# Six gather buffers instead of eight, and a piece and a half of the query weights kept on chip, in a decoder step with PEER experts on one Trainium2 core

## Chip, cores and metric

One NeuronCore of a Trainium2 chip runs the whole program. The metric is the device time of one execution in microseconds, lower is better. A run is one execution; the time before is the median of three.

## What is computed

One layer of a hybrid decoder for 512 prompt tokens and 8 sample tokens (one new token for each of 8 running sequences): modulated RMSNorm, one input projection, a gated delta net (8 heads) beside a forgetting attention (8 heads, for the samples over 2,048 cached positions), an output projection, and then PEER, a mixture of 16,384 tiny experts. Everything is fp32. The part around the change is PEER, cut to what matters:

```python
def one(xb):                                     # xb: normed tokens
    q = (xb @ wq).reshape(blk, 8, 2, 128)        # wq: 1024 x 2048
    s = einsum('thpc,hpnc->thpn', q, subkeys)    # 2 x 128 scores per head
    sv, si = top_k(s, 16)
    cand = sv[:, :, 0, :, None] + sv[:, :, 1, None, :]
    fv, fi = top_k(cand.reshape(blk, 8, 256), 16)
    eidx = ...                                   # 16 experts per token and head
    gate = softmax(fv)
    act = gelu(einsum('thkd,td->thk', pu[eidx], xb)) * gate
    return einsum('thk,thkd->td', act, pv[eidx])
```

Each token thus needs 8 heads x 16 experts, and each expert is a row of 1,024 numbers of `peer_u` and one of `peer_v`. The host lays both side by side as `peer_uv`, rows of 2,048 numbers (8 KB).

## The kernel before, in words

The prompt is cut into 4 tiles of 128 tokens. The first 568 us compute projections, attention, the sample caches and the delta net of tile 0. Then the PEER stage begins and lasts to the end. It is a stream of 520 steps (list `steps_`): 4 tiles x 8 heads x 16 experts, and 8 steps for the samples. A unit is 16 steps, that is one head of one tile.

**One step.** GpSimd (`gather(g)`, line 2650) issues an indirect DMA that fetches for each of 128 tokens its expert's 8 KB row: 128 x 8,192 bytes = 1.0486 MB into buffer `UV[g % UN]`. VectorE (`dot(g)`, line 2386) multiplies the u half with the token's row and sums it (L2398). For two steps at a time, ScalarE makes the gelu (L1476), scales it by the gate (L1482) and writes two 32-column diagonal matrices (L1466), and TensorE (`value_pair`, line 1130) adds the v halves with eight matmuls of 128x512 (L510, `bank<-RING,R` or `bank<-R`). The last matmuls raise `v_used`, one for each step of the pair.

**Landing buffers.** `UV` (line 209) has 8 buffers of 8 KB per partition: six in `RING`, buffer 6 in `R1` from column 12288, buffer 7 in `R2` from column 8192. `gather(g)` waits for `v_used` of step g - 8 (line 2661), and GpSimd does nothing else in this stage; so a buffer is asked for again when TensorE is through with it. A gather into `R1` or `R2` shows in the profile as `R<-in_peer_uv,R`, one into `RING` as `RING<-in_peer_uv,R`.

**The other work of the stage.** While tile i's experts are fetched, the delta net, output projection, norm and queries of tile i + 1 are computed, cut into pieces that are dealt out over the steps (`slots_at`, `post_slots`, `delta_slots`, lines 427 to 464). TensorE does, at each step, first the value pair (even steps), then the pieces of that step. VectorE does first the dot, then a piece of the picking of the best experts for a later unit, then the pieces of the step.

**The query weights.** `wq` is cut into 4 pieces `c` of 512 columns, 2 MB each, stored as 8 row blocks `k` of 128 rows. A piece's lower half is `k` 0 to 3, its upper half 4 to 7. Lower half of piece 0 stays on chip in `WR[0]` (`R1` from 4224). Upper half of piece 0 is kept for tile 0 in `WR[1]` (in `MV`, which holds the token rows later) and is loaded again for tiles 1 to 3. All other weights come through two slots `W[0]`, `W[1]` (`R2` 0 to 8192) in the order of the list `w_parts` (line 414); `weights_in(m)` (line 2886) loads part m when part m - 2 has been used. A tile after the first takes two pieces of the output projection (2 MB each), half of piece 0 (1 MB) and pieces 1 to 3 (2 MB each). SyncE issues these loads on its own queue, in the order in which its program comes to them.

**Before the first gather.** SyncE waits for the delta net of tile 0 (`dS`, 0), loads shift and scale of the norm (`SH2`, `SC2`, in `R2` from 8192), waits for the last attention result (`pt`, 7), and loads the sub-keys (`KN`) and `WR[1]`. VectorE needs `SC2` at L2265, TensorE needs sub-keys and both `WR` from L517 and L510 on (`keys_in`).

Of the kernel before, what the change touches and what calls it, by code (L numbers as in the profile page):

```python
# [56 lines left out]
def hybrid_decoder_step(nc, a, o):  # L57

    ctx = ExitStack()
    with ctx:  # L60
        sems = {}

        def S(name):
            if name not in sems:
                sems[name] = ctx.enter_context(nc.semaphore(name))
            return sems[name]
# [18 lines left out]
        MV = sb("MV", [P, 4, D_MODEL])  # L85
        RQ64 = sb("RQ64", [P, 328])
        R1 = sb("R1", [P, 14336])
# [3 lines left out]
        def part(_t, _at, _n, /, **dims):  # L91
            v = _t[:, _at:_at + _n]
            if not dims:
                return v
            names = list(dims)
            return v.rearrange(f"row ({' '.join(names)}) -> row {' '.join(names)}", **{k: dims[k] for k in names[1:]})
# [83 lines left out]
        W_ROWS = [part(R2, n * 4096, 4096) for n in range(2)]  # L180
        QT = part(R1, 0, 16 * (P + NB), b=16, t=P + NB)
        KEYT = part(R1, 2176, 2048, b=16, n=P)
        SH2, SC2 = part(R2, 8192, 1024), part(R2, 9216, 1024)
        SCS = HT[0:NB, :, 0:2 * P]
        ROWS, SHIFT, SCALE, GATE2, GAIN = HT[64:68, :, 0:P], 0, 1, 2, 3
        GAINS = HT[0:NB, :, 0:P]
# [19 lines left out]
        XS1 = part(R2, 13676, 1024)  # L206
        KN = part(SLOT2, 0, 2048, b=16, c=P)
        FLAT = RING[:, :, :].rearrange("p s n -> p (s n)")
        UV = [part(FLAT, i * 2048, 2048) for i in range(6)] + [part(R1, 12288, 2048), part(R2, 8192, 2048)]
        WR = [part(R1, 4224, 2048, k=4, n=512), MV[:, 0:2, :].rearrange("p n d -> p (n d)").rearrange("p (k n) -> p k n", k=4)]  # L210
        HN = part(R2, 10240, 1024)
        QUARTER = [MV[:, b, :] for b in range(4)]
        WR_ROWS = [part(R1, 4224, 2048), MV[:, 0:2, :].rearrange("p n d -> p (n d)")]
        UN = len(UV)
        FOLD = hide_q[:, 0:32]
        SX = part(R1, 10368, 256, p=2, n=P)
# [130 lines left out]
        def job_done(eng, job):  # L347

            b, use = job_of[job]
            eng.wait_ge(S(f"bank{b}_full"), use)  # L350
# [62 lines left out]

        w_parts = [(0, "wq", c) for c in range(1, 4)]
        for tile in range(1, TILES):
            w_parts += [(tile, "wo", c) for c in range(2)] + [(tile, "wq", c) for c in range(4)]

        def w_slot(eng, i, name, c):

            m = w_parts.index((i, name, c))  # L420
            eng.wait_ge(S(f"w{m % 2}_loaded"), 16 * (m // 2 + 1))
            return W[m % 2]
# [85 lines left out]
        def _(pe):  # L508
# [480 lines left out]
            def query_part(i, c, j, w, ks):  # L989

                n = P if i < TILES - 1 else P + NB
                job = ("qT", i, c, j)
                if ks[0] == 0:
                    take_bank(job, "D")
                b = banks[job_of[job][0]]
                for k in ks:
                    wk = w[:, k, :] if c else WR[0][:, k, :] if k < 4 else (w if i else WR[1])[:, k - 4, :]
                    mm(b[:, 0:n], wk[:, j * P:(j + 1) * P], HT[:, k, i * P:i * P + n], k == 0, k == KT - 1, full(job) if k == KT - 1 else None)

            def scores(i, c):  # L1000
# [76 lines left out]
            def post_slot(i, kind, c=0, j=0, q=0):  # L1077

                if kind == "rest" and c in (0, 1):
                    spread(("shift" if c else "scale", i), SHIFT if c else SCALE)  # L1080
                elif kind == "wo":
                    if c == q == 0:
                        for half in range(2 if j < 4 else 1):
                            job_read(pe, ("oT", j, half))
                        if j == 4:
                            pe.wait_ge(S("sample_attention"), 1)
                    w = w_slot(pe, i, "wo", c) if q == 0 else W[w_parts.index((i, "wo", c)) % 2]
                    mix_part(j, c, w, range(2 * q, 2 * q + 2))
                elif kind == "turn":
                    second_turn(c, j)  # L1090
                elif kind == "wq":
                    if c == j == q == 0:
                        for t in rows_of(i):
                            for half in range(2):
                                job_read(pe, ("h2T", t, half))
                    w = w_slot(pe, i, "wq", c) if j == q == 0 else W[w_parts.index((i, "wq", c)) % 2]
                    query_part(i, c, j, w, range(4 * q, 4 * q + 4))
                elif kind == "score":
                    scores(i, c)
                elif kind == "pairs":  # L1100
                    pair_turns(i, c)
                elif kind == "decay":
                    decay(i, c)
                elif kind == "product":
                    products(i, c)
                elif kind == "solve":
                    solve(i, j, c)
                elif kind in ("X", "Y"):
                    correct(i, j, c, kind)
                elif kind == "wt":  # L1110
                    state_keys(i)
                elif kind == "vn":
                    state_values(i)
                elif kind == "o":
                    state_out(i)
                elif kind == "dS":
                    state_step(i)
                elif kind == "oT":
                    out_turn(i, 0)
# [1555 lines left out]
        def _(sp):  # L2675
            def load(dst, src, sem, **k):
                sp.dma_start(dst, src, **k).then_inc(S(sem), 16)
# [208 lines left out]
            def weights_in(m):  # L2886

                i, name, c = w_parts[m]
                if m >= 2:
                    pi, pname, pc = w_parts[m - 2]  # L2890
                    job_done(sp, ("qT", pi, pc, 3) if pname == "wq" else ("wo", pc, rows_of(pi)[-1]))
                if name == "wq" and c == 0:
                    load(W_ROWS[m % 2][:, 0:2048], wq[0, :, 2048:4096], f"w{m % 2}_loaded")
                else:
                    load(W_ROWS[m % 2], {"wo": w_out, "wq": wq}[name][c], f"w{m % 2}_loaded")

# [3 lines left out]
            sp.wait_ge(S("spilled"), 32 * (TILES - LATE))  # L2900
            load(WR_ROWS[0], wq[0, :, 0:2048], "keys_in")
            job_done(sp, ("dS", 0))
            for i, dst in enumerate((SH2, SC2)):
                load(dst, mod_d[0:1, (3 + i) * D_MODEL:(4 + i) * D_MODEL].to_broadcast([P, D_MODEL]), "mv2_in")
            job_done(sp, ("pt", 7))
            load(KN, a["peer_subkeys"][0].rearrange("h p n c -> n (h p) c"), "keys_in")
            load(WR_ROWS[1], wq[0, :, 2048:4096], "keys_in")
            weights_in(0)
            weights_in(1)
            sp.wait_ge(S("gdn_out"), 1)  # L2910
# [5 lines left out]
            def post_slot(i, kind, c=0, j=0, q=0):  # L2916

                if kind == "wo" and j == rows_of(i)[-1] and q == 3:
                    weights_in(w_parts.index((i, "wo", c)) + 2)
                elif kind == "wq" and j == 3 and q == 1:  # L2920
                    m = w_parts.index((i, "wq", c)) + 2
                    if m < len(w_parts) and (w_parts[m][0] == i or w_parts[m][0] < LATE):
                        weights_in(m)
                elif kind == "tokens" and i == 1 and c == 0:
                    job_done(sp, ("qT", 0, 3, 3))
                    load(ROWS[0:3], mod_d[0:1, 3 * D_MODEL:6 * D_MODEL].rearrange("o (r k c) -> (o r) k c", r=3, k=KT), "rows_in")
                    load(ROWS[3:4], a["final_norm_w"].rearrange("(o k c) -> o k c", o=1, k=KT), "rows_in")
                elif kind == "dS":
                    job_done(sp, ("dS", i))
                    for c in range(2):  # L2930
                        weights_in(w_parts.index((i, "wo", c)))
                elif kind == "oT":
                    job_done(sp, ("oT", i, 0))
                    if i + 1 < TILES:
                        late_in(i + 1)
                    else:
                        load(G1S[0:NB], mod_d[1:9, 2 * D_MODEL:3 * D_MODEL], "g1_in")
                        tile_in(4)
                        for x, dst in enumerate((SH2S, SC2S)):
                            load(dst, mod_d[1:9, (3 + x) * D_MODEL:(4 + x) * D_MODEL].rearrange("b (k c) -> b k c", k=KT), "mv2_in")  # L2940
                        sp.wait_ge(S("state"), 9)
                        for r_ in range(2):
                            store(o["delta_prompt"][0, 0].rearrange("(j a) d e -> a d j e", a=2)[r_], ST[r_ * HD:r_ * HD + HD, :, r_ * HD:r_ * HD + HD], "results_out")
                elif kind == "turn" and c == 4 and j == 0:
                    sp.wait_ge(S("h_ready"), nth_h2(4) + 1)
                    load(G2S[0:NB], mod_d[1:9, 5 * D_MODEL:6 * D_MODEL], "g1_in")
# [84 lines left out]
```

## Time and profile before

| | us |
|---|---|
| median of three runs | 2001.88 |
| lowest, highest | 2001.15, 2002.14 |
| the profiled execution, its own time | 2006.23 |
| its span, first to last instruction | 2004.4 |

| engine | busy us | share of the span |
|---|---|---|
| TensorE (PE) | 1478.0 | 74% |
| VectorE (DVE) | 1330.4 | 66% |
| ScalarE (ACT) | 661.8 | 33% |
| GpSimd (POOL) | 805.4 | 40% |

The profile is of one execution. The row of GB/s cuts the span in 40 slices of 50.1 us; slices 12 to 39 are the PEER stage. In a row of instructions the bracket behind it gives the idle time of the engine just before it and what ended it. In a row of windows, "DMA share" is the mean busy share of the 16 DMA engines, PEclk the granted TensorE clock as a share of 2.4 GHz. A DMA that GpSimd issues is shown with the time that GpSimd took to issue it, not with the time of the transfer.

### The profile page before, as it was taken

What the parts mean: (1) busy time and instruction counts of PE and PEld (TensorE: products, weight loads), DVE (VectorE), ACT (ScalarE), POOL (GpSimd) and SP (SyncE); (2) the same over time, 40 slices, a digit from 0 to 9 for tenths busy, and PEclk for the clock granted to TensorE, in tenths of its full rate; (3) what the DMA queues carried; (4) which work ended last, traced back from release to release, by engine and by line L of the source; (5) the groups of instructions that cost most, each with busy time, mean ns of one, the idle gap of its engine ahead of it and who ended that gap; (6) DMA issues with size and microseconds to landing.
All of it is one profiled execution on the core that took longest, in us unless ns stands there. A gap on an engine that the chain in (4) does not pass through costs nothing. (4 is left out here: it accounts for less than half of the span.)

```text
span 2004.4 us, 30900 instructions
## 1 busy us (share of the span) xinstructions
PE 1478.0 (74%) x10644; PEld 826.6 (41%) x10644; DVE 1330.4 (66%) x3076; ACT 661.8 (33%) x1990; POOL 805.4 (40%) x581
## 2 busy tenths in 40 slices
PE   6999988888977885755698666669866676675444
PEld 4445456566654552432365244335523441121001
DVE  4346666645478876666986666688768568775754
ACT  2211223132124442324454232445433243332322
POOL 0177751203024553435444234544534345344441
PEclk8998999989987997789698777858977895556555
DMA  7387747966779999999999999999999999999996
GB/s 311 120 293 253 242 176 260 338 215 219 251 288 410 418 420 421 422 421 421 415 420 420 422 420 421 419 405 422 420 414 414 422 417 409 407 412 421 422 421 263
DMA packets 130919, 726.93 MB, mean 363 GB/s; under 512 B 17120, under 2 KB 19041, under 8 KB 58437
## 3 DMA queue, kind: packets, MB, share of 16 engines
q0 software_dynamic: 75024, 545.82, 65.9%
q1 hardware_dynamic: 55741, 179.15, 24.6%
q8 instruction: 86, 1.41, 0.3%
q14 instruction: 68, 0.56, 0.1%
HBM read 715.92 MB, written 9.09 MB: 362 GB/s over the span
## 5 line engine op out<-in xcount | busy, mean ns | idle before, releaser
L2663 POOL DMA_INDIRECT RING<-in_peer_uv,R x390 | 464.3, 1191 | 666.6 <-PE bank L510 535.6
L2398 DVE SCALAR_TENSOR_TENSOR RING<-RING,MV 128x1024 f32<-128x1024 f32 x384 | 469.2, 1224 | 290.9 <-DMA RING<-in_peer_uv,R 270.8
L510 PE MATMUL bank<-RING,R 128*32 128x512 f32 (+1 forms) x1560 | 296.9, 815 | 298.9 <-ACT R L1466 282.0
L510 PE MATMUL bank<-R 128*128 128x128 f32 (+5 forms) x2184 | 344.1, 424 | 121.2 <-ACT R L1466 108.8
L510 PEld LDWEIGHTS bank<-R 128*128 128x128 f32 (+4 forms) x2184 | 237.2, 187 | 261.0 <-issue 249.6
L1476 ACT ACTIVATE R<-R 128x2 f32<-128x2 f32 x256 | 52.0, 203 | 775.8 <-DVE RING L2398 661.5
L2663 POOL DMA_INDIRECT R<-in_peer_uv,R x130 | 149.9, 1153 | 196.5 <-PE bank L510 176.1
L510 PEld LDWEIGHTS bank<-RING,R 128*32 128x32 f32 (+1 forms) x1560 | 41.4, 123 | 406.3 <-issue 399.0
L510 PE MATMUL bank<-R,ident 128*32 128x4 f32 (+5 forms) x2500 | 200.8, 273 | 8.8 <-DVE R L2421 2.7
L2398 DVE SCALAR_TENSOR_TENSOR R<-R,MV 128x1024 f32<-128x1024 f32 x128 | 156.5, 1222 | 74.2 <-DMA R<-in_peer_uv,R 64.7
L510 PEld LDWEIGHTS bank<-HT,R 128*128 128x128 f32 x992 | 141.6, 226 | 55.9 <-issue 55.9
L510 PE MATMUL bank<-HT,R 128*128 128x128 f32 (+1 forms) x992 | 153.7, 318 | 0.2 <-issue 0.2
L510 PE MATMUL bank<-HT,RING 128*128 128x512 f32 x320 | 141.9, 601 | 0.0
L510 PEld LDWEIGHTS bank<-R,ident 128*32 128x32 f32 (+3 forms) x2500 | 87.4, 139 | 113.1 <-issue 76.6
L1466 ACT ACTIVATE R<-hide_q,R 128x32 f32<-128x32 f32 x512 | 132.6, 306 | 0.0
L1482 ACT ACTIVATE R<-R 128x1 f32<-128x1 f32 x512 | 122.8, 286 | 8.4
L2604 POOL TENSOR_TENSOR MV<-MV,RING 128x2048 f32<-128x2048 f32 x16 | 72.7, 4553 | 87.9 <-DMA RING<-samp_d 53.5
L510 PE MATMUL bank<-RING,HT 128*8 128x128 f32 (+3 forms) x688 | 95.8, 353 | 5.1 <-ACT HT L1215 3.7
L510 PE MATMUL bank<-R,HT 128*128 128x64 f32 (+5 forms) x416 | 89.9, 382 | 1.2 <-DVE small L1962 0.7
L510 PEld LDWEIGHTS bank<-HT,RING 128*128 128x128 f32 x320 | 60.8, 193 | 72.6 <-issue 72.5
L2604 POOL TENSOR_TENSOR R<-R,RING 128x2048 f32<-128x2048 f32 x16 | 72.1, 4520 | 21.8 <-DMA R<-in_cache_k 21.8
L517 PE MATMUL bank<-ident,R 128*128 128x128 f32 (+2 forms) x242 | 47.0, 345 | 37.3 <-DVEq L2224 11.8
(336 smaller groups left out, 1740.9 us busy)
## 6 DMA issues: line engine op xcount, KB each, us to landing
R<-in_peer_wq SPq DMA_DIRECT2D x12, 2048.0 KB
RING<-in_w_mod SPq DMA_DIRECT2D x11, 2048.0 KB, 9.3
R<-in_cache_v SPq DMA_DIRECT2D x84, 256.0 KB, 3.7
MV<-in_cache_k SPq DMA_DIRECT2D x64, 256.0 KB, 3.9
R<-in_cache_k SPq DMA_DIRECT2D x64, 256.0 KB, 3.6
R<-in_w_out SPq DMA_DIRECT2D x6, 2048.0 KB
MV<-in_cache_v SPq DMA_DIRECT2D x44, 256.0 KB, 4.0
RING<-in_peer_uv,R POOLq DMA_INDIRECT x390
```

The lines of the kernel that those rows point to most:

```text
L510: i = nc.tensor.matmul(out, lhsT, rhs, start=start, stop=stop, **k)
L517: i = nc.tensor.transpose(out, in_, ident[0:n, 0:n])
L1466: A(DG[:, k % 4, :], FOLD, ACT.Copy, scale=AG[:, n % 4, s_:s_ + 1]).then_inc(S("diagonal"), 1)
L1476: A(AG[:, n % 4, s_:s_ + 2], DOT[:, n % 4, s_:s_ + 2], ACT.Gelu).then_inc(S("gelu"), 1)
L1482: A(AG[:, n % 4, x:x + 1], AG[:, n % 4, x:x + 1], ACT.Copy, scale=GATS[:, n % 4, x:x + 1]).then_inc(S("weights"), 1)
L2398: V.scalar_tensor_tensor(u, u, 1.0, QUARTER[s_ % 4], ALU.mult, ALU.mult, accum_out=DOT[:, n % 4, s_:s_ + 1]).then_inc(S("dots"), 1)
L2604: T(k, k, QB[:, n // 4 % 2:n // 4 % 2 + 1, :].to_broadcast([P, 4, 512]), ALU.mult).then_inc(S("kprod"), 1)
L2663: nc.gpsimd.indirect_dma_start(UV[g % UN], None, a["peer_uv"][0], bass.IndirectOffsetOnAxis(ap=idx, axis=0)).then_inc(S(f"uv_in{g % UN}"), 16)
```

## The change

Landing buffers 6 and 7 go. In their places stand, for good, the upper half of piece 0 (`R2` from 8192) and the lower half of piece 1 (`R1` from 12288). `UN` becomes 6, so a gather waits for step g - 6. Piece 0 is not loaded again for tiles 1 to 3, and of piece 1 only the upper half is. Shift and scale move to `MV`; so SyncE loads them after its wait for (`pt`, 7), and the load of the upper half of piece 0 comes before that wait. TensorE waits once for the new half of piece 1 (`wq1_in`).

```diff
-        SH2, SC2 = part(R2, 8192, 1024), part(R2, 9216, 1024)
+        SH2, SC2 = MV[:, 0, :], MV[:, 1, :]
...
-        UV = [part(FLAT, i * 2048, 2048) for i in range(6)] + [part(R1, 12288, 2048), part(R2, 8192, 2048)]
-        WR = [part(R1, 4224, 2048, k=4, n=512), MV[:, 0:2, :].rearrange("p n d -> p (n d)").rearrange("p (k n) -> p k n", k=4)]
+        UV = [part(FLAT, i * 2048, 2048) for i in range(6)]
+        WR = [part(R1, 4224, 2048, k=4, n=512), part(R2, 8192, 2048, k=4, n=512), part(R1, 12288, 2048, k=4, n=512)]
...
-            w_parts += [(tile, "wo", c) for c in range(2)] + [(tile, "wq", c) for c in range(4)]
+            w_parts += [(tile, "wo", c) for c in range(2)] + [(tile, "wq", c) for c in range(1, 4)]
...
+                if i == 0 and c == 1 and j == ks[0] == 0:
+                    pe.wait_ge(S("wq1_in"), 16)
                 for k in ks:
-                    wk = w[:, k, :] if c else WR[0][:, k, :] if k < 4 else (w if i else WR[1])[:, k - 4, :]
+                    wk = WR[2 * c + k // 4][:, k % 4, :] if 2 * c + k // 4 < 3 else w[:, k - 4 * (c == 1), :]
...
-                if name == "wq" and c == 0:
-                    load(W_ROWS[m % 2][:, 0:2048], wq[0, :, 2048:4096], f"w{m % 2}_loaded")
+                if name == "wq" and c == 1:
+                    load(W_ROWS[m % 2][:, 0:2048], wq[1, :, 2048:4096], f"w{m % 2}_loaded")
...
             job_done(sp, ("dS", 0))
+            load(WR_ROWS[1], wq[0, :, 2048:4096], "keys_in")
+            job_done(sp, ("pt", 7))
             for i, dst in enumerate((SH2, SC2)):
                 load(dst, mod_d[0:1, (3 + i) * D_MODEL:(4 + i) * D_MODEL].to_broadcast([P, D_MODEL]), "mv2_in")
-            job_done(sp, ("pt", 7))
             load(KN, a["peer_subkeys"][0].rearrange("h p n c -> n (h p) c"), "keys_in")
-            load(WR_ROWS[1], wq[0, :, 2048:4096], "keys_in")
+            load(WR_ROWS[2], wq[1, :, 0:2048], "wq1_in")
...
-                elif kind == "wq" and j == 3 and q == 1:
+                elif kind == "wq" and c and j == 3 and q == 1:
```

## Rows read from the trace of the kernel before

**Rows 1.** The page: span, and GB/s in 40 slices

```profile
span 2004.4 us, 30900 instructions
...
GB/s 311 120 293 253 242 176 260 338 215 219 251 288 410 418 420 421 422 421 421 415 420 420 422 420 421 419 405 422 420 414 414 422 417 409 407 412 421 422 421 263
```

**Rows 2.** The page's DMA issues: tile, queue, count, KB each

```profile
R<-in_peer_wq SPq DMA_DIRECT2D x12, 2048.0 KB
...
RING<-in_peer_uv,R POOLq DMA_INDIRECT x390
```

**Rows 3.** Window of the PEER stage: busy us by engine, PEclk, DMA share, GB/s

```profile
568.00:1990.00 1422.00, 975.34 (x7255) 515.50 (x7253) 1014.43 (x2510) 535.19 (x1729) 614.23 (x520) 0.75 1.00 414
```

**Rows 4.** Timeline: a load of query weights (841.42), and VectorE behind it

```profile
841.42 0.33 SPq L2677 DMA_DIRECT2D R<-in_peer_wq  x1
...
851.22 1.23 DVE L2398 SCALAR_TENSOR_TENSOR RING<-RING,MV 128x1024 f32<-128x1024 f32 x1 [4.71 <-DMA RING<-in_peer_uv,R]
```

**Rows 5.** Timeline of a quiet stretch: dot, value pair, and the gather it frees

```profile
1859.16 1.23 DVE L2398 SCALAR_TENSOR_TENSOR RING<-RING,MV 128x1024 f32<-128x1024 f32 x1 [0.84 <-DMA RING<-in_peer_uv,R]
...
1861.71 1.94 PE L510 MATMUL bank<-RING,R 128*32 128x512 f32 x8 [3.04 <-ACT R L1466]
...
1863.93 0.94 POOL L2663 DMA_INDIRECT RING<-in_peer_uv,R  x1 [1.49 <-PE bank L510]
```

**Rows 6.** Timeline of a quiet stretch near 700 us: dot, and the gather freed

```profile
700.22 1.23 DVE L2398 SCALAR_TENSOR_TENSOR RING<-RING,MV 128x1024 f32<-128x1024 f32 x1 [0.91 <-DMA RING<-in_peer_uv,R]
...
704.12 0.94 POOL L2663 DMA_INDIRECT RING<-in_peer_uv,R  x1 [1.86 <-PE bank L510]
```

**Rows 7.** Timeline of the start: first gather, first value pair, ninth gather, its dot

```profile
568.35 0.99 POOL L2663 DMA_INDIRECT RING<-in_peer_uv,R  x1 [69.05 <-DVEq L2326]
...
594.66 1.93 PE L510 MATMUL bank<-RING,R 128*32 128x512 f32 x8 [7.18 <-ACT R L1466]
...
597.37 1.74 POOL L2663 DMA_INDIRECT RING<-in_peer_uv,R  x1 [19.34 <-PE bank L510]
...
603.69 1.23 DVE L2398 SCALAR_TENSOR_TENSOR RING<-RING,MV 128x1024 f32<-128x1024 f32 x1 [1.64 <-DMA RING<-in_peer_uv,R]
```

**Rows 8.** Windows at the start, columns as in rows 3

```profile
595.00:600.00 5.00, 5.00 (x28) 3.48 (x21) 5.00 (x16) 1.33 (x6) 2.32 (x2) 0.60 0.28 77
601.00:602.00 1.00, 1.00 (x13) 0.49 (x11) 1.00 (x4) 0.41 (x3) 0.00 (x0) 1.00 0.93 393
```

**Rows 9.** GpSimd's timeline: first gather of a pair, before and after late stretches

```profile
619.53 1.54 POOL L2663 DMA_INDIRECT RING<-in_peer_uv,R  x1 [0.32 <-PE bank L510]
...
672.95 0.94 POOL L2663 DMA_INDIRECT R<-in_peer_uv,R  x1 [2.28 <-PE bank L510]
...
973.70 1.01 POOL L2663 DMA_INDIRECT RING<-in_peer_uv,R  x1 [1.75 <-PE bank L510]
...
987.39 1.31 POOL L2663 DMA_INDIRECT RING<-in_peer_uv,R  x1 [2.44 <-PE bank L510]
...
1024.54 0.94 POOL L2663 DMA_INDIRECT RING<-in_peer_uv,R  x1 [3.00 <-PE bank L510]
...
1063.47 1.96 POOL L2663 DMA_INDIRECT R<-in_peer_uv,R  x1 [2.15 <-PE bank L510]
...
1642.73 0.94 POOL L2663 DMA_INDIRECT RING<-in_peer_uv,R  x1 [1.86 <-PE bank L510]
...
1651.94 1.56 POOL L2663 DMA_INDIRECT R<-in_peer_uv,R  x1 [6.12 <-PE bank L510]
...
1741.08 0.94 POOL L2663 DMA_INDIRECT RING<-in_peer_uv,R  x1 [2.73 <-PE bank L510]
...
1749.20 1.73 POOL L2663 DMA_INDIRECT RING<-in_peer_uv,R  x1 [5.87 <-PE bank L510]
```

**Rows 10.** Timeline before the first gather: SyncE after (`pt`, 7), and VectorE with `SC2`

```profile
537.99 0.87 SPq L2677 DMA_DIRECT2D RING<-in_peer_subkeys  x1
...
545.38 0.69 DVE L2265 TENSOR_TENSOR R<-R 128x512 f32<-128x512 f32 x1
```

More of the change, by code:

```diff
@@ L208, in hybrid_decoder_step @@
         FLAT = RING[:, :, :].rearrange("p s n -> p (s n)")
-        UV = [part(FLAT, i * 2048, 2048) for i in range(6)] + [part(R1, 12288, 2048), part(R2, 8192, 2048)]
-        WR = [part(R1, 4224, 2048, k=4, n=512), MV[:, 0:2, :].rearrange("p n d -> p (n d)").rearrange("p (k n) -> p k n", k=4)]
+        UV = [part(FLAT, i * 2048, 2048) for i in range(6)]
+        WR = [part(R1, 4224, 2048, k=4, n=512), part(R2, 8192, 2048, k=4, n=512), part(R1, 12288, 2048, k=4, n=512)]
         HN = part(R2, 10240, 1024)
         QUARTER = [MV[:, b, :] for b in range(4)]
-        WR_ROWS = [part(R1, 4224, 2048), MV[:, 0:2, :].rearrange("p n d -> p (n d)")]
+        WR_ROWS = [part(R1, 4224, 2048), part(R2, 8192, 2048), part(R1, 12288, 2048)]
         UN = len(UV)
@@ L1095, in post_slot @@
                                 job_read(pe, ("h2T", t, half))
-                    w = w_slot(pe, i, "wq", c) if j == q == 0 else W[w_parts.index((i, "wq", c)) % 2]
+                    w = None if c == 0 else w_slot(pe, i, "wq", c) if j == q == 0 else W[w_parts.index((i, "wq", c)) % 2]
                     query_part(i, c, j, w, range(4 * q, 4 * q + 4))
```

## The prediction, made before the changed kernel was run

> **What bounds the kernel now.** First the page's row of GB/s: from slice 12 on it stands at 405 to 422, where it was 120 to 338 before [rows 1]. The reader is to see a plateau: something is full. Next the window of the PEER stage: the DMA engines' share is 1.00, while TensorE works 975 and VectorE 1014 of 1422 us [rows 3]. So the stage is set by bytes. They are mostly gathers: 520 (390 of them into `RING`, [rows 2], the others into the two buffers that the change removes) of 1.0486 MB each. At the plateau's 421 GB/s [rows 1] a gather takes 2.49 us, a pair 4.98 us. Last the chain in a quiet stretch: VectorE waits for a landing (dot at 1859.16, its idle time ended by the DMA), the value pair starts at 1861.71, and GpSimd, released by it, asks for the next gather at 1863.93 [rows 5]. That is 4.77 us from landing to request where a value pair takes 1.94 us; at full TensorE clock, near 700 us, it is 704.12 - 700.22 = 3.90 us [rows 6]. Nothing of this is late as long as the DMA queues still hold gathers when the next request arrives. How many they hold is what the buffers decide.
>
> **Part 1, bytes removed.** Twelve loads of 2 MB of `wq` [rows 2] become eight, and by the lines of the program five of 1 MB become seven: 29 MB become 23. The difference is 6 MB, 2 MB in each of tiles 1 to 3, that is 3 x 2.097 MB / 421 GB/s = 14.9 us. Are they on the path? The load of 841.42 is the one that tile 1 no longer needs, and two like it follow in tiles 2 and 3; the dot of 851.22 behind it waited 4.71 us for its gather [rows 4], and VectorE had nothing else to do. The queues share the same engines, so a weight byte pushes a gather byte back. **-14.9 us.** SyncE issues one load fewer per tile, 0.33 us each, off the path.
>
> **Part 2, the start.** The picks of unit 0 allow 8 gathers from 568.35 on, but the first value pair starts at 594.66, and the ninth gather at 597.37 [rows 7]. Between them the DMA engines run dry: 77 GB/s from 595 to 600 [rows 8]. What sets 594.66 is the picking and the gates on VectorE, not a landing, so it stays. With six buffers the engines run dry two gathers earlier, and those two are still to be fetched afterwards: 2 x 2.49 = **+5.0 us**. This is certain unless the engines had time to spare later, which [rows 3] excludes.
>
> **Part 3, late releases.** Here is the unknown. When the second gather of a pair has landed, six buffers leave four gathers in the queues, 4 x 2.49 = 9.96 us of work; eight left 14.9. From that go the 4.77 or 3.90 us until the next request, and the time from request to flowing data. The trace has that once with empty queues: requested at 597.37, the data come at nearly full rate, 393 GB/s, from 601 on [rows 8], and the dot starts at 603.69, 6.32 us after the request, 3.8 more than the bytes need [rows 7]. I take 3.7. So the slack is 9.96 - 4.77 - 3.7 = 1.5 us, or 2.4 at full clock; call it 2.0. It was 6.5 to 7.3. A quiet stretch still fits. A stretch in which TensorE or VectorE has too many pieces does not: its lateness beyond the slack becomes idle DMA time. GpSimd's rows show the lateness against 4.98 us a pair [rows 9]: 619.53 to 672.95 is 10 pairs, 53.4 us for 49.8, late by 3.6; 973.70 to 987.39 is 2 pairs, late by 3.7, and the same pieces come again from 1329.13 to 1342.82; 1024.54 to 1063.47 is 7 pairs, late by 4.1; 1642.73 to 1651.94 is one, late by 4.2; 1741.08 to 1749.20 one, late by 3.1. Less 2.0 each: 1.6, 1.7, 1.7, 2.1, 2.2, 1.1. I halve the first and the fourth, as they are spread over many pairs, in which a pause of the gathers gives the engines time back: 0.8 + 1.7 + 1.7 + 1.0 + 2.2 + 1.1 = **+8.5 us.** The bounds: none of it, if data flow as soon as the queues need them; without halving and with a slack of 1.5, six times 0.5 more, 13.4. Where weights are loaded (750 to 880, 1104 to 1230, 1456 to 1600) releases are late too, but 4 to 5 MB of weights, 10 us or more, fill the queues meanwhile. I cost that at nothing; with one load fewer the cover may be short by 2 us in each of the three, so the upper bound is 13.4 + 6 = 19.4.
>
> The Trainium skill, page "DMA: Bandwidth & Descriptors", section "Anatomy of one DMA — SWDGE (gpsimd) path", gives a fixed 2.0 us plus bytes over 436 GB/s. That makes 4.4 us of one gather, where the trace has 6.32 [rows 7]. By the page, as an estimate, the slack would be 3.2 to 4.1 us, part 3 some 2 us and the sum -8. The measurement decides, and the page is no term here.
>
> **Moved pieces, with one answer.** Shift and scale are now loaded after (`pt`, 7), at about 538.0 [rows 10], ahead of the sub-keys. VectorE needs them at 545.38, 7.4 us later; a 1 MB transfer took 6.3 us from empty queues [rows 7]. Nothing, with 1 us to spare; if that cover fails, the first gather moves by what is missing, 1 or 2 us. Sub-keys and `WR[1]` were 2 MB after 538; shift, scale and sub-keys are 2 MB too, so `keys_in` is complete at the same time. The lower half of piece 1 stands ahead of a load of 1 MB less. TensorE's wait for it comes behind all of piece 0. `weights_in` for piece 2 now follows the output projection directly, which is earlier. No engine gets more instructions.
>
> **The sum.** -14.9 + 5.0 + 8.5 = -1.4 us. The profiled execution took 2006.23, 4.35 above the median; it would take 2004.8, and the median 2001.88 - 1.4 = 2000.5. About 0.2%, 4 us, can be told from no change here; this cannot.
>
> **The rivals.**
>
> *The slack suffices.* Part 3 is 0 to 5 us, if the queues need a request less early than 597.37 shows; those were empty queues, and a queue that is not yet empty may hide part of the start. For it: in the quiet windows nothing is lost. Against it: slices 26, 32 and 33 fall to 405, 409 and 407 GB/s [rows 1], so even eight buffers lose something. Time: 2001.88 - 9.9 to -4.9, **1992 to 1997**. Chance 0.34.
>
> *The slack is gone in quiet stretches too.* Place: the stretch from 1640 on, where the value pair takes 1.94 us. Six gathers make a cycle of three pairs, landing, dot, value pair, request, data. It decides where request to data is over 9.96 - 4.77 = 5.2 us. At 5.8, say because the gathers of a pair slow each other, each cycle is 0.6 us longer; 350 us / 14.9 = 23 cycles, +14 us. With parts 1 to 3: **2014**. Short of that, part 3 at its upper bound gives -14.9 + 5.0 + 19.4 = +9.5, 2011. For it: the margin is 1.5 us, and requests take GpSimd up to 1.96 instead of 0.94 us [rows 9]. Against: the measured 3.8. Together 0.24.
>
> *The removed loads were hidden.* Then part 1 is 0 and the time 2001.88 + 13.5 = **2015**. Against it stands the 4.71 us of waiting [rows 4]. Chance 0.04.
>
> *The forecast*, within 4 us: 0.38.
>
> **How the numbers follow.** Predicted 2000.5. The lower end is part 3 at nothing, 1992.0, with a microsecond below. The upper end is 2011.4 from the upper bound, with a microsecond above; the two slow cases beyond it, 0.1, are left out, and as much below. Faster by over 0.2%: 0.34; within: 0.38; slower: 0.28. The likeliest case's own range is 1998 to 2006.
>
> **What would show it.** Right: `R<-in_peer_wq` x8 with 2048 KB and x7 with 1024; 6 MB fewer read; no gather into `R`; first value pair still near 594.7; empty queues from about 590 instead of 595; 421 GB/s in 700 to 750 and 1800 to 1980, where a pair still takes 4.98 us; windows around 980, 1336, 1648 and 1747 well below 400 GB/s, each for some microseconds. VectorE's waits for gathers become longer in all, dots no longer start late behind a stock of landed buffers. Wrong: quiet stretches below 415 GB/s (part 3's slack), or no dip at the late places (the first rival), or a first gather later than 570.

## The result, and the profile after

The changed kernel took 2037.79 us in the median of 4 runs (2029.43 to 2045.34), the kernel before 2001.52 beside it: a ratio of 1.0179, 95% interval 1.0153 to 1.0205. The forecast was 2000.5 with a range up to 2012.5. It is slower by 36 us, outside the range and on the other side of no change. The runs of the changed kernel also lie 16 us apart, those of before in this set 2.4 (8 to 13 in the later sets, of 9 to 25 runs).

The profiled execution took 2033.66 us, that of before 2006.23; so what follows accounts for 27 us, where the medians differ by 36. From its page: the span, the GB/s in 40 slices, and the DMA issues (tile, queue, count, KB each, median us to landing).

```profile
span 2031.9 us, 30895 instructions
...
GB/s 307 128 305 225 250 183 271 343 187 246 268 269 372 422 417 422 417 409 417 382 402 400 417 402 419 411 390 398 410 413 405 418 381 399 385 406 400 396 403 291
...
HBM read 709.63 MB, written 9.09 MB: 354 GB/s over the span
...
R<-in_peer_wq SPq DMA_DIRECT2D x8, 2048.0 KB, 12.4
...
RING<-in_peer_uv,R POOLq DMA_INDIRECT x520, 9.5
```

Eight whole loads of `wq` are left of twelve, and all 520 gathers go to `RING`, as the diff says [rows 2]. The plateau of [rows 1] is no plateau any more: from slice 12 to the last but one (slices are counted from 0) it stands at 372 to 422 where it was 405 to 422, and the slices near the end, which have nothing but gathers, stand at 385 to 406. Windows of the same execution (columns as in rows 3: us, then busy us of PE, PEld, DVE, ACT and POOL, PEclk, DMA share, GB/s):

```profile
568.00:2017.00 1449.00, 971.23 (x7216) 510.14 (x7215) 1012.85 (x2493) 533.32 (x1726) 595.86 (x517) 0.75 0.99 401
1800.00:1900.00 100.00, 53.36 (x286) 10.43 (x286) 63.55 (x154) 26.83 (x99) 44.10 (x39) 0.60 0.99 395
1900.00:1980.00 80.00, 31.85 (x256) 6.44 (x256) 49.79 (x109) 26.22 (x90) 34.34 (x31) 0.50 1.00 404
```

The engines' work is what it was [rows 3]: TensorE 971 for 975 us, VectorE 1013 for 1014. What grew is VectorE's waiting for gathers, 386.9 us in 368 waits where before it was 270.8 + 64.7 = 335.5 us in 316 (us, times, longest; the changed kernel, then the two rows of the kernel before from 568 to 1990):

```profile
DVE RING L2400 <- DMA RING<-in_peer_uv,R: 386.9, 368, 6.1
...
DVE RING L2398 <- DMA RING<-in_peer_uv,R: 270.8, 244, 4.9
DVE R L2398 <- DMA R<-in_peer_uv,R: 64.7, 72, 4.5
```

The reader should distrust one column. The DMA share is 0.99 to 1.00 in windows that move 395 to 404 GB/s, as in those of before at 421: a packet that takes long counts as busy.

Where the time went is read best from the landings of the 520 gathers. This table is worked out from the landing of every gather in both profiles, in us from one landing to another (the slots of another tile's work end with the 384th):

```
landings       1-17  17-65  -129   -193   -257   -321   -385   -449   -520    sum
before         51.7  121.0  190.6  163.1  191.4  164.3  190.0  164.7  178.5  1415.3
after          59.4  123.1  187.0  172.6  188.7  169.8  187.6  174.6  184.8  1447.6
```

The difference is +32.3 us (the first gather of this execution is issued 4.3 us earlier, which makes the 27 us above), though 6.3 MB, 14.9 us, are gone. So some 47 us are new: 7.7 at the start; in the three stretches with weight loads (columns -129, -257, -385) 8.7 saved instead of 14.9, so 6.2; in the other stretches of the first three tiles 2.1 + 9.5 + 5.5 = 17.1; in the last tile 16.2. The prediction had 5.0 + 8.5.

### The profile page after: what moved, and what is told of

It reads as the page before. It is cut to its first block and busy times, and to the rows that moved or that the text cites. A ratio compares the mean times of both kernels' runs of the same rounds, so it can differ in the third digit from the quotient of the medians.

```text
span 2031.9 us, 30895 instructions
## 1 busy us (share of the span) xinstructions
PE 1473.1 (72%) x10644; PEld 822.3 (40%) x10644; DVE 1333.1 (66%) x3076; ACT 660.4 (33%) x1990; POOL 790.0 (39%) x581
## 5 line engine op out<-in xcount | busy, mean ns | idle before, releaser
L2665 POOL DMA_INDIRECT RING<-in_peer_uv,R x520 | 598.9, 1152 | 914.6 <-PE bank L510 765.1
L2400 DVE SCALAR_TENSOR_TENSOR RING<-RING,MV 128x1024 f32<-128x1024 f32 x512 | 626.4, 1225 | 398.9 <-DMA RING<-in_peer_uv,R 388.4
L510 PE MATMUL bank<-RING,R 128*32 128x512 f32 (+1 forms) x2080 | 392.7, 809 | 431.4 <-ACT R L1468 424.3
L510 PEld LDWEIGHTS bank<-RING,R 128*32 128x32 f32 (+1 forms) x2080 | 55.4, 123 | 585.0 <-issue 571.2
L510 PEld LDWEIGHTS bank<-R 128*128 128x128 f32 (+3 forms) x1664 | 226.1, 210 | 100.9 <-issue 90.3
L510 PE MATMUL bank<-R 128*128 128x128 f32 (+5 forms) x1664 | 251.4, 308 | 6.7 <-ACT R L1436 3.0
L510 PEld LDWEIGHTS bank<-RING,HT 128*8 128x8 f32 (+1 forms) x688 | 52.4, 128 | 44.8 <-issue 43.1
L517 PEld LDWEIGHTS bank<-ident,R 128*128 128x128 f32 (+2 forms) x242 | 34.9, 178 | 79.0 <-issue 23.1
## 6 DMA issues: line engine op xcount, KB each, us to landing
R<-in_w_out SPq DMA_DIRECT2D x6, 2048.0 KB, 14.9
```

The costliest lines, as they stand in the source:

```text
L510: i = nc.tensor.matmul(out, lhsT, rhs, start=start, stop=stop, **k)
L517: i = nc.tensor.transpose(out, in_, ident[0:n, 0:n])
L2400: V.scalar_tensor_tensor(u, u, 1.0, QUARTER[s_ % 4], ALU.mult, ALU.mult, accum_out=DOT[:, n % 4, s_:s_ + 1]).then_inc(S("dots"), 1)
L2665: nc.gpsimd.indirect_dma_start(UV[g % UN], None, a["peer_uv"][0], bass.IndirectOffsetOnAxis(ap=idx, axis=0)).then_inc(S(f"uv_in{g % UN}"), 16)
```

## Experiments

Eleven runs of ten kernels, in three sets, the kernel before timed beside each set. Ratios are to the kernel before.

**1. The two halves of the change, apart.** First only the buffers go, then only the loads (of the second, where the missing halves would be read, the query projection multiplies by a resident half, so its part of the output is another one).

```diff
-        UV = [part(FLAT, i * 2048, 2048) for i in range(6)] + [part(R1, 12288, 2048), part(R2, 8192, 2048)]
+        UV = [part(FLAT, i * 2048, 2048) for i in range(6)]
```

> The kernel before with two landing buffers fewer and every load kept: the landing half of the change alone. Theory A (the six buffers do the harm: with two gathers fewer requested ahead, the 16 DMA engines have no store of queued packets, so each late request and each disturbed engine is paid for in full, in quiet stretches too): the loss of the change comes back without the bytes saved, 2037.8 + 14.9 = about 2052 us, between 2045 and 2060, and the quiet stretch 1800 to 1900 us moves under 405 GB/s. Rival B (the loss comes from the moved and regrouped weight loads, from the piece kept in other places or from the waits of the load queue): only the start and the late releases that the prediction counted are left, 2001.5 + 13.5 = about 2015 us, and the quiet stretch stays at 420 GB/s.

```diff
-            w_parts += [...] + [(tile, "wq", c) for c in range(4)]
+            w_parts += [...] + [(tile, "wq", c) for c in range(1, 4)]
...
-                    wk = w[:, k, :] if c else WR[0][:, k, :] if k < 4 else (w if i else WR[1])[:, k - 4, :]
+                    wk = WR[0][:, k, :] if k < 4 and c < 2 else WR[0 if i else 1][:, k - 4, :] if c == 0 else w[:, k - 4 * (c == 1), :]
...
-                if name == "wq" and c == 0:
-                    load(W_ROWS[m % 2][:, 0:2048], wq[0, :, 2048:4096], f"w{m % 2}_loaded")
+                if name == "wq" and c == 1:
+                    load(W_ROWS[m % 2][:, 0:2048], wq[1, :, 2048:4096], f"w{m % 2}_loaded")
...
```

> The kernel before with all eight landing buffers, and the weight loads cut as the change cuts them: piece 0 is not loaded again and of piece 1 the upper half alone is loaded. Where the missing halves would be read, the matmuls read the resident half (so part of the query projection is computed with other weights). It loads 3 x 2.097 + 1.05 = 7.3 MB less than the kernel before. Theory A: the bytes come off at the rate of the stage, 7.3 MB / 421 GB/s = 17.4 us, about 1984 us (1981 to 1988). Rival C (the weight loads were hidden, so their removal brings nothing): 2001 us.

Six buffers with every load: 2054.2 us, ratio 1.0266 (1.0244 to 1.0288). Eight buffers with fewer loads: 1984.8 us, 0.9921 (0.9897 to 0.9945). Both times are as theory A said. Its sign in the quiet stretch was missed: in the profile of the first, which is the fastest of its four executions (2042.4), the window from 1800 to 1900 moves 415 GB/s, not under 405, and the loss shows elsewhere (401 GB/s from 1250 to 1440). So one window of one profile does not tell where the loss lies; the run with the hold in the last tile, below, does. The parts add up: 1.0266 - 1 is +53 us, 1.0179 - 1 is +36, and the difference of 17 is the price of the bytes, about the 14.9 of part 1. The loads were worth what the prediction gave; the buffers cost four times what it gave (13.5).

**2. The place, or the time of the request?** The kernel before, eight places and all loads; only GpSimd's wait is moved, so that a request comes as if there were six buffers, first in all tiles, then in the last alone.

```diff
-                if g >= UN:
-                    pool.wait_ge(S("v_used"), g - UN + 1)
+                if g >= 6:
+                    pool.wait_ge(S("v_used"), g - 6 + 1)
```

> The kernel before with all eight landing buffers and all its loads, but each gather waits for the value step six gathers back, not eight: the time of the request is that of the six-buffer kernel, while places and loads are those of before. Theory A (the time of the request alone does it): as the run with six buffers and the same loads, 2054 us, 2044 to 2060. Rival F (the harm is in where or how closely the gathers land: six neighbouring places reused at once, reads and writes in the same places): 2001 to 2010 us, with 2.5 us for the start.

```diff
+                held = 6 if n >= 3 * PH else UN
                 if g >= UN:
-                    pool.wait_ge(S("v_used"), g - UN + 1)
+                    pool.wait_ge(S("v_used"), g - held + 1)
```

> The same hold in the last tile alone (from the 385th gather on), where no other tile's work lies between the steps. Theory A: only that tile loses, the 16 us that the landings from the 385th on took more in the changed kernel (359.4 against 343.2 us in the profiles): 2001.5 + 16 = about 2018 us, 2012 to 2022. Rival G (the hold costs only where the engines' other work makes releases late, so in the tiles before): 2001 to 2005 us.

2055.6 us, 1.0257 (1.0216 to 1.0298), and 2018.3 us, 1.0083 (1.0064 to 1.0102). Both are in theory A's ranges. That settles the cause: one number in one wait makes the whole loss, with every buffer still there, and 17 us of it belong to the last tile, which has hardly anything but gathers, dots and value pairs. The last gathers of the second kernel, from 1800 on, against the same kernel's first tiles:

```profile
930.00:1090.00 160.00, 123.92 (x999) 72.88 (x991) 129.68 (x312) 77.87 (x228) 75.54 (x63) 0.84 1.01 419
1250.00:1440.00 190.00, 147.57 (x1196) 87.64 (x1196) 148.44 (x366) 90.05 (x270) 90.14 (x75) 0.83 1.01 416
1800.00:1980.00 180.00, 81.96 (x474) 14.47 (x466) 110.31 (x243) 48.59 (x179) 78.11 (x69) 0.55 1.00 402
```

The windows in which TensorE and VectorE work hardest keep 416 to 419 GB/s with eight requests ahead; the idlest falls to 402 with six. The same three windows of the changed kernel show 397, 402 and 399, of the kernel before 419, 416 and 421.

**3. Seven.** One buffer fewer with every load; then the changed kernel with `R1` at 12288 as seventh buffer, so that piece 0 stays and piece 1 is streamed whole, 3.1 MB fewer than before.

```diff
+        UV = [part(FLAT, i * 2048, 2048) for i in range(6)] + [part(R1, 12288, 2048)]
+        WR = [part(R1, 4224, 2048, k=4, n=512), part(R2, 8192, 2048, k=4, n=512)]
...
+                    wk = w[:, k, :] if c else WR[k // 4][:, k % 4, :]
...
```

> The kernel before with one landing buffer fewer (seven) and every load kept, beside the run with six and the same loads (2054 us). Theory A (a late request costs only where the lead of a request over the landing before it falls under 7.5 us, as the sorted landings of the six-buffer traces show; the seventh buffer adds one landing of 2.5 us to every lead): most of the loss is already away, 2001.5 + 2.5 (start) + about 10 = about 2014 us, 2008 to 2020. Rival E (each buffer is worth the same, half of the loss of two): 2001.5 + 52 / 2 = about 2028 us, 2024 to 2034.

> The changed kernel with the place of the third resident half given back as a seventh landing buffer: piece 0 of the query weights stays, piece 1 is streamed whole, 3.1 MB fewer loaded than before. Theory A: the run with seven buffers and the same loads, less 3.1 MB / 421 GB/s = 7.5 us, about 2007 us. Rival E: about 2020 us.

> The kernel with seven buffers and piece 0 resident again, to see whether its gain holds in another set of runs: ratio 0.998 (0.997 to 0.9995), 1998 us beside 2002. If the gain was chance: ratio 1.000 or above.

Seven with every load: 2004.9 us, ratio 1.0009 (0.9992 to 1.0025). That is outside theory A's own 2008 to 2020, on the good side: the seventh buffer takes away practically all of the loss, so the curve is not a slope but an edge: about +2 us from eight to seven, which is within its interval of nothing, and +50 from seven to six. Seven with piece 0 resident: 1998.1 us, 0.9983 (0.9972 to 0.9995), and in another set 1996.5 us, 0.9972 (0.9960 to 0.9983). The first is 9 us below its expectation, which was built on 2014 for seven buffers; against the 2004.9 measured, the 3.1 MB brought 6.7 us where 7.5 were expected. The repetition came out as expected. This kernel is 3 to 6 us faster than the kernel before, and 40 faster than the changed one. Its windows, the same three:

```profile
930.00:1090.00 160.00, 127.21 (x1002) 72.64 (x994) 129.53 (x312) 78.39 (x227) 77.76 (x63) 0.82 1.01 416
1250.00:1440.00 190.00, 149.37 (x1196) 88.85 (x1196) 148.11 (x363) 88.60 (x263) 88.98 (x74) 0.82 1.01 411
1800.00:1980.00 180.00, 86.10 (x512) 20.99 (x512) 111.01 (x238) 51.00 (x189) 72.80 (x69) 0.56 1.01 419
```

**4. Earlier requests without a buffer.** Gelu, diagonals and value matmuls for each step by itself, so that the first of two buffers comes free one landing earlier: with six buffers, and with eight as the control.

```diff
-                elif n is not None and g % 2 == 0:
-                    value_pair(g, n, s_)
+                elif n is not None and s_ == 0 and n % PH == 0:
+                    value_steps(g, n, s_, 2)
+                n, s_ = step_at(g + 1)
+                if n is not None and n < SAMPLES and (n % PH or s_ > 1):
+                    value_steps(g + 1, n, s_, 1)
...
-                if e % 2 and n is not None:
-                    gelu(e // 2)
+                if n is not None and n < SAMPLES:
+                    gelu(e, 1)
+                elif n is not None and e % 2:
+                    gelu(e - 1, 2)
```

> The changed kernel, with the Gelu, the diagonals and the value matmuls of each step issued as soon as that step's dot is done, not for two steps together; only the first two steps of a tile stay together. Of each two buffers the first is released about one landing (2.5 us) earlier, and the requests no longer come in pairs. Theory A (requests that come too late for the engines' queues): the lead of a request over the landing before it rises from 5 to 7 us to 7 to 8.5 us, where the trace of the changed kernel shows no excess, so most of the 42 us return: 1995 to 2010 us, and the quiet stretch goes back over 415 GB/s. Rival D (with six buffers the engines are disturbed by other things, instruction fetches or slow packets, whatever the time of the request): within 5 us of the changed kernel, 2030 to 2040 us.

> The kernel before with the same single steps, as the control of the run before this one. Theory A: with eight buffers the requests are early enough outside the late releases, so at most the 13 us that its trace lost in mid-stage are to be had: 1990 to 2001 us. Rival D: no change, 2001 us; slower than 2003 us if the added Gelus or the matmuls issued one step earlier cost something of themselves.

2025.1 us, 1.0115 (1.0097 to 1.0132), and 2018.0 us, 1.0081 (1.0064 to 1.0097). The first missed both of its times; only the quiet stretch did what was expected, 417 GB/s from 1800 to 1900. The second missed the times of theory A and of rival D and came out as its last clause had it, slower than 2003. It tells why the first returned so little: with eight buffers single steps cost 16 us of themselves. By shape, the value matmuls of the kernel before from 568 to 1990 (count, then busy us, mean ns of one, idle time before them and its releasers):

```profile
L510 PE MATMUL bank<-RING,R 128*32 128x512 f32 x1536 | 283.5, 817 | 296.5 <-ACT R L1466 282.0 <-issue 14.5
...
L510 PE MATMUL bank<-R 128*32 128x512 f32 x504 | 91.4, 803 | 106.4 <-ACT R L1466 105.5 <-issue 0.8
```

and of eight buffers with single steps, then VectorE's waits for TensorE in it:

```profile
L510 PE MATMUL bank<-RING,R 128*32 128x512 f32 x1520 | 468.2, 722 | 150.1 <-ACT R L1469 149.3
L510 PE MATMUL bank<-R 128*32 128x512 f32 x504 | 157.2, 706 | 98.6 <-ACT R L1469 98.4
```

```profile
DVE R L2418 <- PE bank L510: 35.4, 14, 7.4
DVE R L2411 <- PE bank L510: 33.0, 6, 8.5
DVE R L2134 <- PE bank L510: 23.8, 12, 4.7
```

As many matmuls take 625 instead of 375 us of TensorE, since those of two steps had run beside each other: 2040 of some 814 ns in 375 us are 4.4 at a time, 2024 of some 718 ns in 625 us are 2.3. In the tiles with other work this makes TensorE late, VectorE waits 92 us for it in these three rows (12 in the three largest such rows of the kernel before), and the releases come later than before: the window 930 to 1090 falls from 419 to 405 GB/s. In the last tile, where TensorE has room, the idea works: with six buffers the landings from the 385th on take 344.5 us, where the changed kernel needs 359.4 and the kernel before 343.2. Requests there, in the kernel with six buffers and single steps:

```profile
1857.64 1.05 PE L510 MATMUL bank<-RING,R 128*32 128x512 f32 x4 [1.43 <-ACT R L1471]
1857.82 1.23 DVE L2408 SCALAR_TENSOR_TENSOR RING<-RING,MV 128x1024 f32<-128x1024 f32 x1 [1.24 <-DMA RING<-in_peer_uv,R]
...
1858.97 0.94 POOL L2673 DMA_INDIRECT RING<-in_peer_uv,R  x1 [1.55 <-PE bank L510]
...
1860.30 1.23 DVE L2408 SCALAR_TENSOR_TENSOR RING<-RING,MV 128x1024 f32<-128x1024 f32 x1 [1.25 <-DMA RING<-in_peer_uv,R]
```

One request for each landing, and a landing every 2.48 us. So single steps in the last tile alone, two together elsewhere:

```diff
+        def alone(g):
+            n, s_ = steps_[g]
+            return 3 * PH <= n < SAMPLES and (n % PH or s_ > 1)
...
```

> The changed kernel with single steps (Gelu, diagonal and value matmuls as soon as the step's dot is done) in the last tile alone, where no other tile's work lies between the steps; two steps together everywhere else. In the trace with single steps everywhere the landings of that tile (from the 385th on) took 344.5 us, against 359.4 in the changed kernel and 343.2 before. Theory A (the quiet tile lost its 16 us by late requests): 2037.8 - 15 = about 2023 us, 2018 to 2027, and the granted clock may rise there. Rival D (the last tile's loss is not in the time of the requests): 2034 to 2041 us.

> The run with seven buffers and piece 0 resident, with single steps in the last tile: the version that could beat both kernels. Theory A: the last tile's landings back to 343 us, and elsewhere the loss of the seven-buffer run less the 7.5 us of bytes: about 2003 us, 1998 to 2008. Rival E (each buffer worth the same): about 2012 us, of which the last tile returns 8 us of a loss of 26.

With six buffers 2030.3 us (2020.5 to 2034.6), 1.0124 (1.0093 to 1.0155): half of what was expected, above its range and below the rival's. In its profile the last tile took 351.5 us, 8 less than in the changed kernel and 7 more than in the kernel with single steps everywhere. Of these 7, 4.8 lie in the first 16 landings (from the 385th to the 401st: 46.0 us, with single steps everywhere 41.2, in the changed kernel 45.7). The first six requests there still wait for steps of the tile before, which go in pairs in this kernel, and the 389th gather is requested only 0.2 us ahead of the landing that it follows. No run tests this, and the other 2 us are open. With seven 1998.5 us, 0.9987 (0.9974 to 0.9999), in the range, but nothing beyond the run without it: with seven buffers there is nothing left for an earlier request to save.

## Why the prediction was wrong

**Part 1 was right.** The bytes are on the path: 0.9921 for 7.3 MB is 16 us (11 to 21) where 17.4 were worked out.

**Part 2 was right in kind, and 2.7 us short in this pair of profiles.** The profiles that begin with eight buffers differ among themselves by as much: the 16 landings after the first take 51.3 to 54.2 us in four of them, with six buffers and steps in pairs 59.4 to 59.6 in three. Start of the changed kernel, from its timeline: first gather, first value pair, seventh and ninth gather, and the seventh's dot [rows 7].

```profile
564.05 0.99 POOL L2665 DMA_INDIRECT RING<-in_peer_uv,R  x1 [66.64 <-DVEq L2328]
...
590.35 1.94 PE L510 MATMUL bank<-RING,R 128*32 128x512 f32 x8 [14.65 <-ACT R L1468]
592.56 0.94 POOL L2665 DMA_INDIRECT RING<-in_peer_uv,R  x1 [21.32 <-PE bank L510]
...
598.19 1.23 DVE L2400 SCALAR_TENSOR_TENSOR RING<-RING,MV 128x1024 f32<-128x1024 f32 x1 [3.65 <-DMA RING<-in_peer_uv,R]
599.00 1.23 POOL L2665 DMA_INDIRECT RING<-in_peer_uv,R  x1 [4.19 <-PE bank L510]
```

and two windows there (columns as in rows 3):

```profile
590.00:595.00 5.00, 4.65 (x22) 3.02 (x23) 4.54 (x14) 1.63 (x8) 1.94 (x2) 0.53 0.18 29
...
600.00:602.00 2.00, 2.00 (x18) 1.04 (x16) 0.82 (x1) 1.97 (x5) 1.16 (x2) 1.00 0.61 152
```

The first value pair comes 26.3 us after the first gather in both kernels, so the picks set it, as said. But the next pair's release is at 599.00, after only two requests, and the engines run short a second time, 152 GB/s from 600 to 602. How much of the 2.7 us that makes no run shows. The moved loads cost nothing that shows: the first gather is at 564.05, and between 560 and 572 us in the profiles with and without them.

**Part 3 is the step that failed**, at "So the slack is 9.96 - 4.77 - 3.7 = 1.5 us, or 2.4 at full clock" and the sentence built on it, "A quiet stretch still fits". The first two terms hold: the first request of a pair is then 5.2 us ahead of the landing that it follows (call this distance its lead), and the second, which comes 1.24 us later for a landing 2.49 us later, 6.4. In the last tile of the changed kernel the median of that lead is 6.3 us, with a tenth below 4.8. The third does not. 3.7 us was read from one gather into empty queues [rows 7, 8], and taken for the lead from which on nothing is lost. As the time of one such gather it was, if anything, long: in the changed kernel the seventh, also into empty queues, is requested at 592.56 and its dot starts at 598.19 (rows above), 5.6 us, 3.1 more than its bytes need. What failed is its use as a threshold in a running stream. Sorting the landings of the changed kernel with no weight traffic by their lead shows the excess over 2.485 us instead (worked out from the trace):

```
lead, us        under 4   4-5    5-6    6-7.5   over 7.5
landings           13      22    110     208      93
excess, us       12.6    10.6   17.2     8.1     -0.2
```

There is no threshold at 3.7. A landing with 4 to 5 us of lead already costs 0.5 us, one with 5 to 6 still 0.16, and there are 110 of those. The same sum for the kernel before is 11 us, over leads that are nearly all above 7.5; the difference of 37 is what the first section found outside the start, 39. The two other kernels with six gathers ahead, sorted the same way, have more of it at short leads: under 5 us, 37 landings cost 26 of 43 us (six buffers, all loads) and 53 cost 33 of 48 (eight held as six), and one of 5 to 6 costs 0.09 and 0.04. The sorting alone shows only that loss and short lead go together; that the time of the request makes the loss is shown by the held kernels. The prediction charged lateness at six places; in truth the standing lead of a six-buffer cycle lies so near to where time is lost that a small delay falls at once into the dear columns: 35 to 53 landings under 5 us carry about half of the loss or more, and over a hundred of 5 to 6 a part of the rest. One such case, from the timeline of the changed kernel's last tile:

```profile
1885.33 1.94 PE L510 MATMUL bank<-RING,R 128*32 128x512 f32 x8 [4.46 <-ACT R L1468]
...
1888.05 0.94 POOL L2665 DMA_INDIRECT RING<-in_peer_uv,R  x1 [4.48 <-PE bank L510]
...
1892.68 1.23 DVE L2400 SCALAR_TENSOR_TENSOR RING<-RING,MV 128x1024 f32<-128x1024 f32 x1
...
1895.96 1.23 DVE L2400 SCALAR_TENSOR_TENSOR RING<-RING,MV 128x1024 f32<-128x1024 f32 x1 [1.45 <-DMA RING<-in_peer_uv,R]
```

and the windows inside it (PE busy us alone, PEclk, DMA share, GB/s):

```profile
1883.00:1888.00 5.00, 1.94 (x8) 0.50 1.01 424
1889.00:1890.00 1.00, 0.00 (x0) 0.50 1.14 377
1890.00:1891.00 1.00, 0.35 (x4) 0.50 0.73 238
1891.00:1892.00 1.00, 1.00 (x8) 0.50 0.88 369
```

The request of 1888.05 is 4.6 us ahead of the landing at 1892.7 that it should follow; by the prediction 0.9 us to spare. Its own landing comes 3.3 us after that one, not 2.5, and some 2 us behind the request the engines fall to 238 GB/s.

What shows for it over the whole last tile (from the 385th landing on, worked out from the records of gathers and of their 8 KB packets, whose median is 0.31 us):

```
                                    lead median  a tenth below  packets over 0.6 us  the tile, us
before (8)                             10.4          9.4          71 of 17013          343.2
7 buffers, all loads                    8.3          6.7          80 of 17146          344.5
7 buffers, piece 0                      8.2          6.5          72 of 17150          343.1
6, single steps everywhere              7.9          5.9          99 of 17176          344.5
6, single steps in the last tile        7.9          5.5         144 of 17170          351.5
changed kernel (6)                      6.3          4.8         296 of 17163          359.4
6 buffers, all loads                    6.2          4.9         238 of 17182          356.5
8, held as six everywhere               6.0          4.8         248 of 17185          355.7
8, held as six in the last tile         6.2          4.8         268 of 17159          360.4
```

The time follows the lead, and above all its lowest tenth: at 6.5 us and over at most 1.3 us are lost, at 4.8 to 4.9 us 12 to 17. It does not follow it closely: the two rows with single steps have nearly the same leads and lie 7 us apart. In the changed kernel the packets over 0.6 us take, beyond the usual 0.31 us each, 12 us per engine, before 3; the engines' idle time between packets makes 6 us, before 3. Whether a packet is slow because its engine had just run out of queued work, or something else makes both, no run here separates.

**The rivals.** "The slack is gone in quiet stretches too" had the right place and sign, and its price of 14 us for that stretch was near the 16.2 measured (12 to 17 in the four profiles with six gathers ahead there and steps in pairs); even so its total, 2014, is 24 us too low. The other tiles lost 17.1 us where some 5 of part 3's 8.5 were meant for them, and 6.2 more beside the weight loads, costed at nothing (the bound, "short by 2 us in each of the three", had nearly that, 6). That the gathers of a pair slow each other, the reason it supposed, no run tests. Its condition, request to data over 5.2 us, was the right question; the answer came from the one measured case instead of from the spread. The first rival, that the slack suffices, had 0.34 and has nothing for it. The slices that it names, 32 and 33, are 33 and 34 in the count that begins with 0, by which 26 is right; nothing rests on that.

**The views of "what would show it"** did their work: "quiet stretches below 415 GB/s (part 3's slack)" is what the profile shows, 395 and 404 from 1800 on.

## What to carry to other kernels

Count buffers by the standing lead of a request over the landing that it must follow, in the slowest quiet cycle, and ask for at least a landing of margin beyond what a single transfer shows (here 3.1 to 3.8 us beyond its bytes, where nothing was lost from some 6.5 us of lead on); a transfer into empty queues gives the least lead, not a sufficient one. Before a buffer is given away, hold the requests back by a single changed wait: that one-line run, with the buffers still there, would have told the loss here before any buffer moved, 1.0257 against the 1.0266 of taking the buffers away. Near the edge one place decides: seven buffers and two resident halves are faster than before, six buffers and three halves slower.

## What was not expected of the hardware

- The edge itself: with the same loads eight, seven and six gathers ahead give 2002, 2005 and 2054 us.
- The DMA share is blind to it: 1.00 at 399 GB/s and 1.01 at 421 (window 1800 to 1980, changed kernel and before).
- The value matmuls of two steps cost TensorE as much as those of one: eight in 1.07 us (at 601.01 in the changed kernel), four in 1.05 us (at 1857.64 with single steps), both at a granted clock of 1.00.
- A theory that fell: in the kernel before, the 16 engines drift apart in the last tile, so that the last of them reports a gather 3.9 us (median) after their mean, and in the changed kernel 1.2. It looked like a store that absorbs disturbances, and the first expectations say so. But from eight to seven buffers the distance falls to 1.6 to 1.9 us and at most 2 us of time are lost; from there to six it falls to 1.1 to 1.2, and 50 are. And with six buffers and single steps it is 1.4, and the last tile loses 1.3 us. So the loss does not come with the drift.
